# Projection to the queries and keys of differential attention, in both layers, by Strassen's seven half products

## The reference

```python
p = h @ w_in[l][:, diff columns]                     # 768 columns: q, k, v
q, k, v = jnp.split(p, 3, axis=-1)                   # 256 each
q, k = rope_2d(q of latents), rope_2d(k of latents)  # context tokens stay unrotated
amap = softmax(q1 k1 * scale) - lam * softmax(q2 k2 * scale)
o = amap @ v
```

## Time and profile before

| | us |
|---|---|
| median of 3 runs (2094.13 to 2097.17) | 2095.87 |
| the profiled execution | 2094.3 |
| its span | 2092.2 |
| TensorE busy (matmul) | 1942.3 (93%) |
| VectorE busy | 721.6 (34%) |
| ScalarE busy | 519.1 (25%) |

### The profile page before, as it was taken

The page is one execution under the profiler, slowest core; times in us unless marked ns, Lnnn a source line. Parts: engine busy times, 40 slices in busy tenths (PEclk is TensorE's granted clock), DMA queues, the critical chain, the costliest instruction groups (busy, mean ns, idle before and its releaser), DMA issues. The chain is left out here.

```text
span 2092.2 us, 25952 instructions
## 1 busy us (share of the span) xinstructions
PE 1942.3 (93%) x10858; PEld 934.4 (45%) x10858; DVE 721.6 (34%) x1335; ACT 519.1 (25%) x1020; POOL 186.9 (9%) x216
## 2 busy tenths in 40 slices
PE   5998999989989999999999999999898998888886
PEld 2656565544433333333334866655445333232222
DVE  2258565372431110111113476563624111111113
ACT  4146552452300000000003255524321100000012
POOL 1300000120011111212012000001100000000000
PEclk9999999999999999999999999999999999999999
DMA  9520304222289999999999223024419999999996
GB/s 351 147 81 1 141 1 152 90 105 96 82 343 401 393 399 395 394 401 393 402 395 301 111 82 141 1 90 153 165 61 357 395 408 408 408 409 409 409 409 261
DMA packets 164805, 530.64 MB, mean 254 GB/s; under 512 B 11016, under 2 KB 19538, under 8 KB 164690
## 3 DMA queue, kind: packets, MB, share of 16 engines
q1 hardware_dynamic: 149344, 489.49, 60.0%
q0 software_dynamic: 15120, 39.43, 6.1%
q10 hardware_dynamic: 226, 0.07, 0.0%
HBM read 507.98 MB, written 20.97 MB: 253 GB/s over the span
## 5 line engine op out<-in xcount | busy, mean ns | idle before, releaser
L3267 PE MATMUL ps<-ring,arena 128*64 128x512 f32 x1040 | 233.2, 597 | 13.6 <-DMA ring<-in_w_up 8.8
L3267 PE MATMUL ps<-arena 128*64 128x512 f32 x720 | 165.0, 604 | 3.6 <-DMA arena<-in_w_gate 3.2
L3267 PEld LDWEIGHTS ps<-ring,arena 128*64 128x64 f32 x1040 | 72.1, 137 | 161.6 <-issue 141.3
L3093 PE MATMUL ps<-ring,arena 128*128 128x512 f32 x320 | 141.6, 597 | 1.0 <-ACT arena L1442 0.6
L2366 DVE TENSOR_TENSOR arena<-arena,ps 128x512 f32<-128x512 f32 x32 | 22.0, 688 | 280.1 <-ACT arena L1487 280.1
L3316 PE MATMUL ps<-ring,arena 128*64 128x512 f32 x496 | 112.4, 596 | 5.8 <-DMA ring<-in_w_down 5.8
L2476 PE MATMUL ps<-arena,ring 128*128 128x256 f32 (+1 forms) x384 | 110.4, 447 | 2.5 <-DMA ring<-in_w_in 2.5
L1487 ACT ACTIVATE arena<-ps 128x512 f32<-128x512 f32 x32 | 19.1, 597 | 373.4 <-PE ps L3267 373.4
L3316 PE MATMUL ps<-arena 128*64 128x512 f32 x432 | 97.9, 595 | 5.2 <-DMA arena<-in_w_down 4.5
L1066 ACT ACTIVATE arena<-ps 128x768 f32<-128x768 f32 (+6 forms) x111 | 79.9, 724 | 88.0 <-PE ps L2494 45.3
L3267 PEld LDWEIGHTS ps<-arena 128*64 128x64 f32 x720 | 50.4, 139 | 107.0 <-issue 100.3
(11 more groups left out here) (417 smaller groups left out, 2821.8 us busy)
## 6 DMA issues: line engine op xcount, KB each, us to landing
ring<-in_w_up SPq DMA_DIRECT2D x33, 2048.0 KB, 14.7
ring<-in_w_gate SPq DMA_DIRECT2D x32, 2048.0 KB, 21.1
ring<-in_w_down SPq DMA_DIRECT2D x30, 2048.0 KB, 23.0
ring<-in_ada_w SPq DMA_DIRECT2D x24, 2048.0 KB, 9.9
arena<-in_w_down SPq DMA_DIRECT2D x19, 2048.0 KB, 23.2
arena<-in_w_gate SPq DMA_DIRECT2D x18, 2048.0 KB, 22.5
arena<-in_w_up SPq DMA_DIRECT2D x12, 2048.0 KB, 13.6
ring<-in_w_in SPq DMA_DIRECT2D x6, 2048.0 KB, 14.0
```

Of the source, the lines that this page charges most:

```text
L3093: ins = mm(o[:, hf * 512:(hf + 1) * 512], mix, wo[hf][:, k, :], start=k == 0, stop=k == KD - 1)
L3267: ins = mm(px[0][hf * 64:hf * 64 + 64, col:col + 512], xl[e % 2][:, at:at + CAP_L], w[c][:, hf * 512:hf * 512 + 512], start=b + c == 0, st ...
```

## The change

The four blocks are taken as two pairs, `p` = 0 with blocks 0 and 2 (a query block and a key block, 256 channels apart), `p` = 1 with blocks 1 and 3. Tokens are halved (384 and 384 in layer 0, 256 and 256 in layer 1), features too. For each pair there are seven half products of four feature blocks each. In this document they are numbered as they are issued, with a for pair 0 and b for pair 1:

1. first weights' half, first features, by first tokens; copied out by ScalarE
2. the same with the second features, into the same place once that copy is done
3. weight sum `SQ[1]` by token sum `TQ[1]`
4. `SQ[2]` by `TQ[2]`, onto the same place, once VectorE has taken product 3 (sums 11 and 12)
5. `SQ[0]` by `TQ[0]`
6. plain weights by `TQ[3]`
7. `SQ[3]` by plain tokens, in the place of 5 (sums 14 and 17)

The order is 1a 1b 2a 2b 3a 3b 4a 4b, 5a 6a 7a, 5b, the turn of block 2, 6b 7b, the turn of block 0; then the values, with the turns of blocks 3 and 1 behind the first (or only) values' job. VectorE makes eight sums of inputs first (four of tokens, four of weights), then sums results as products come, six to a pair. The rotations go in the order 2, 0, 3, 1: block 2's before pair 1 is finished, the other three behind it. ScalarE scales query blocks in place in SBUF. The first scores wait for two rotated blocks where they waited for three. Job numbers and tiles are as before.

```diff
+        def half_counts(l, conv):
+            return (10 * (2 * l + conv), (QK_SUMS + CONV_SUMS) * l + conv * QK_SUMS, 8 * l + conv * (4 if l else 6))
+        def qk_ready(l, m):
+            _, sums0, out0 = half_counts(l, 0)
+            if l and m >= 2:
+                return S["half_sums"], sums0 + (15 if m == 2 else 18)
+            return S["half_out"], out0 + ((3, 4)[m] if l else (4, 6, 3, 5)[m])
...
-                for m in range(4):
-                    j, scale = jb("qk") + m, DQ ** -0.5 if m < 2 else 1.0
-                    act.wait_ge(*J.filled(j))
-                    ins = act.activation(QK[:, m, CTX:TOK], J.tile(j)[:, CTX:TOK], ACT.Copy, scale=scale)
+                products0, sums0, _ = half_counts(l, 0)
+                _, _, EQ, _ = qk_sums_homes(l)
+                for p in range(2):
+                    act.wait_ge(S["half_products"], products0 + p + 1)
+                    act.activation(EQ[p], J.tile(jb("qk") + 2 * p)[:, 0:qk_half(l)], ACT.Copy).then_inc(S["half_out"], 1)
+                for m in (2, 0, 3, 1):
+                    scale = DQ ** -0.5 if m < 2 else 1.0
+                    if m < 2:
+                        act.wait_ge(*J.freed(jb("qk") + 2 * m + 1))
+                        ins = act.activation(QK[:, m, CTX:TOK], QK[:, m, CTX:TOK], ACT.Copy, scale=scale)
+                    elif l == 0:
+                        act.wait_ge(S["half_sums"], sums0 + (15 if m == 2 else 18))
                     if l == 0:
-                        ins = context_heads_out(QH if m < 2 else KH, m % 2, J.tile(j)[:, 0:CTX], scale)
-                    ins.then_inc(*J.free(j))
+                        ins = context_heads_out(QH if m < 2 else KH, m % 2, QK[:, m, 0:CTX], scale)
+                    if m < 2 or l == 0:
+                        ins.then_inc(S["half_out"], 1)
...
+                qk_sum(TQ[0], qk_rows(0, 1), qk_rows(0, 0), ALU.subtract)
+                qk_sums_done(1)
+                qk_sum(TQ[1], qk_rows(4, 1), TQ[0], ALU.subtract)
+                dve.wait_ge(ring_full[n4 % RING], ring_turns(n4) * 16)
+                qk_sum(SQ[0], qk_weights(1, 0), qk_weights(1, 4))
+                qk_sums_done(3)
+                qk_sum(SQ[1], SQ[0], qk_weights(0, 0), ALU.subtract)
+                qk_sum(SQ[2], qk_weights(0, 0), qk_weights(1, 0), ALU.subtract)
+                qk_sum(TQ[2], qk_rows(4, 1), qk_rows(0, 1), ALU.subtract)
+                qk_sums_done(4)
+                qk_sum(SQ[3], qk_weights(0, 4), SQ[1], ALU.subtract)
+                qk_sum(TQ[3], qk_rows(4, 0), TQ[1], ALU.subtract)
+                for p in range(2):
+                    dve.wait_ge(S["half_out"], out0 + p + 1)
+                    dve.wait_ge(S["half_products"], products0 + 3 + p)
+                    qk_sum(qk_out(p, 0), EQ[p], qk_tile(p, 0, 0))
+                for p in range(2):
+                    dve.wait_ge(S["half_products"], products0 + 5 + p)
+                    qk_sum(EQ[p], EQ[p], qk_tile(p, 0, 1))
+                for p in range(2):
+                    qk_sums_done(11 + p)
+                    dve.wait_ge(*J.filled(jb("qk") + 2 * p))
+                    TT(UQ[p], EQ[p], qk_tile(p, 0, 1), ALU.add).then_inc(*J.free(jb("qk") + 2 * p))
...
+                def qk_late(p):
+                    dve.wait_ge(*J.freed(jb("qk") + 2 * p))
+                    dve.wait_ge(S["half_products"], products0 + 7 + 2 * p)
+                    qk_sum(qk_out(2 + p, 1), UQ[p], qk_tile(p, 1, 0))
+                    qk_sum(EQ[p], EQ[p], qk_tile(p, 1, 0))
+                def qk_early(p):
+                    dve.wait_ge(S["half_products"], products0 + 8 + 2 * p)
+                    qk_sum(qk_out(2 + p, 0), UQ[p], qk_tile(p, 1, 1))
+                def qk_last(p):
+                    qk_sums_done((14, 17)[p])
+                    dve.wait_ge(*J.filled(jb("qk") + 2 * p + 1))
+                    TT(qk_out(p, 1), EQ[p], qk_tile(p, 1, 0), ALU.add).then_inc(*J.free(jb("qk") + 2 * p + 1))
+                qk_late(0)
+                qk_early(0)
+                qk_last(0)
+                qk_late(1)
+                for i, m in enumerate((2, 0, 3, 1)):
+                    if i == 1:
+                        qk_early(1)
+                        qk_last(1)
+                    dve.wait_ge(*qk_ready(l, m))
                     lat = QK[:, m, CTX:TOK]
                     TT(rope_t[0], lat, kc(K_COS, SEQ), ALU.mult)
                     j = jb("rot") + m
                     dve.wait_ge(*J.filled(j))
...
-                    pe.wait_ge(*J.freed(jb("qk") + m))
+                    pe.wait_ge(*qk_ready(l, m))
...
+                def qk_product(p, i, hf, a, b, k0=None):
+                    o = J.tile(jb("qk") + 2 * p + i)[:, 512 * hf:512 * hf + n]
+                    for k in range(4):
+                        if k0 is not None:
+                            h_ready(k0 + k)
+                        ins = mm(o, a[:, k, :], b[:, k, :], start=k == 0, stop=k == 3)
+                    return ins
+                def of_qk_pair(x, p):
+                    return SQ[x][:, :, P * p:P * p + P]
+                for p in range(2):
+                    pe.wait_ge(*J.empty(jb("qk") + 2 * p))
+                    qk_product(p, 0, 0, qk_weight(p, 0, 0), qk_rows(0, 0), 0 if p == 0 else None).then_inc(S["half_products"], 1)
+                for p in range(2):
+                    pe.wait_ge(S["half_out"], out0 + p + 1)
+                    qk_product(p, 0, 0, qk_weight(p, 0, 4), qk_rows(4, 0), 4 if p == 0 else None).then_inc(S["half_products"], 1)
+                pe.wait_ge(S["half_sums"], sums0 + 4)
+                for p in range(2):
+                    qk_product(p, 0, 1, of_qk_pair(1, p), TQ[1]).then_inc(S["half_products"], 1)
+                for p in range(2):
+                    pe.wait_ge(S["half_sums"], sums0 + 11 + p)
+                    qk_product(p, 0, 1, of_qk_pair(2, p), TQ[2]).then_inc(*J.fill(jb("qk") + 2 * p))
+                for p in range(2):
+                    pe.wait_ge(*J.empty(jb("qk") + 2 * p + 1))
+                    qk_product(p, 1, 0, of_qk_pair(0, p), TQ[0]).then_inc(S["half_products"], 1)
+                    if p:
+                        quarter_turned(2)
+                    qk_product(p, 1, 1, qk_weight(p, 1, 4), TQ[3]).then_inc(S["half_products"], 1)
+                    pe.wait_ge(S["half_sums"], sums0 + (14, 17)[p])
+                    qk_product(p, 1, 0, of_qk_pair(3, p), qk_rows(4, 1)).then_inc(*J.fill(jb("qk") + 2 * p + 1))
+                quarter_turned(0)
                 w = arrived(wb + 5)
                 wv = w
                 if l:
                     token_major(jb("v"), w[:, :, 0:256], range(CT, CT + 2), 256, 256)
                     quarter_turned(3)
+                    quarter_turned(1)
                     pe.wait_ge(*J.freed(jb("kc")))
                     pe.wait_ge(*J.freed(jb("vc")))
                 else:
                     token_major(jb("v"), w[:, :, 0:256], range(0, 4), 256, 256)
                     quarter_turned(3)
+                    quarter_turned(1)
                     token_major(jb("v") + 1, w[:, :, 0:256], range(4, 6), 256, 256)
                     pe.wait_ge(*J.freed(jb("v") + 1))
-                pe.wait_ge(*w_.next(S["qk_roped"], 3))
+                pe.wait_ge(*w_.next(S["qk_roped"], 2))
```

More of the change, by code:

```diff
@@ L599, in xr, with qk_half, qk_sums_homes @@
             return X[:, at:at + n]
+        QK_SUMS, CONV_SUMS = 18, 22
+        def half_counts(l, conv):
[5 more added lines that the diff above has]
+            return S["half_out"], out0 + ((3, 4)[m] if l else (4, 6, 3, 5)[m])
+        def qk_half(l):
+            return (TOK - query_tiles(l)[0] * P) // 2
+        def qk_sums_homes(l):
+            n = qk_half(l)
+            th = [view(x, k=4) for x in (ar(a0, 4 * n), ar(a0 + 4 * n, 4 * n), X[:, 4 * TOK:4 * TOK + 4 * n],
+                                         X[:, 4 * TOK + 4 * n:4 * TOK + 8 * n])]
+            sw = [view(ar(a2 + 1024 + i * 1024, 1024), k=4) for i in range(3)] + [view(ar(a0 + 8 * n if l else 21504, 1024), k=4)]
+            e = a1 + 4 * TOK + (512 if l else 0)
+            return th, sw, [ar(e + p * n, n) for p in range(2)], [ar(e + (2 + p) * n, n) for p in range(2)]
         HT = TOK // 2
@@ new lines, in qk_weights, with qk_sum, qk_out, qk_tile @@
+                def qk_weights(half, k0):
+                    return ringv(n4)[:, k0:k0 + 4, 256 * half:256 * half + 256]
+                def qk_sum(to, x, y, op=ALU.add):
+                    TT(to, x, y, op).then_inc(S["half_sums"], 1)
+                def qk_out(m, half):
+                    return QK[:, m, c0 + half * n:c0 + half * n + n]
+                def qk_tile(p, i, hf):
+                    return J.tile(jb("qk") + 2 * p + i)[:, 512 * hf:512 * hf + n]
+                if l:
+                    for b in range(4):
+                        dve.wait_ge(*J.freed(jb("hl") + b))
+                    dve.wait_ge(s_xst, 16 * nq)
@@ new lines, in _, with qk_weight, qk_rows @@
```

(10 more changed lines are left out.)

23 lines of the change are left out of this document (10 added, 13 removed).

## The result

| | before | after |
|---|---|---|
| median | 2095.6 (4 executions) | 2111.88 (4, from 2108.27 to 2113.92) |
| the profiled execution | 2094.3 | 2113.68 |
| its span | 2092.2 | 2111.5 |
| granted clock, mean of the span | 0.988 | 0.982 |
| VectorE busy | 721.6 | 753.0 |

The ratio is 1.0076, with a 95% interval from 1.0058 to 1.0094: slower by 16.3 us. The forecast said slower, 2104.9, with a range to 2109.5; the direction is right, the time lies outside the range. Seven half products for eight save work, and the kernel pays for it with holes and with clock.

A forecast was written before the change was run, and what follows sets the result against it. TensorE's stream was taken as the bound at the projection, if nothing else came late. Products and holes gave +0.7 and +5.7, low clock +2.6: +9.0 on a median of 2095.9, hence 2104.9 us, range 2098.5 to 2109.5.

The forecast's parts named there:

- The products and the stream: Projection in both layers: 14 half products for four blocks save 5.2 us in layer 0 and 3.4 in layer 1.
- The holes: TensorE waits before values, their second part, product 4a and first scores: 1.5 and 4.3 us; 0.3, 2.1, 2.4 and 4.3.
- The sum of +6.4: First scores later by 0.7 us in layer 0 and 5.7 in layer 1, saved products and holes together, without low clock.
- The clock behind the long holes: Half clock behind the 4.3 us hole of each layer, costing 1.3 us each, within bounds of 0 and 1.6.
- rival 3: All four holes bring low clock, also those of 2.1 and 2.4 us in layer 1: +12.8, 2108.7 us; chance 15%.
- +9.0: Whole kernel: +6.4 from products and holes plus 2.6 for low clock, if all holes of this length pay.
- My row of 2.45 us: Trace row at 42.7 us: half clock behind a 2.45 us hole, read as evidence that the 4.3 us holes lower the clock.
- the clock's term of the sum: Low clock behind the two 4.3 us holes, one in each layer, adds 2.6 us to +6.4.
- 1 (stream alone, -6.5): TensorE's stream alone decides, turned tiles being free in time before values and scores: 6.5 us faster, 2089.4; chance 5%.
- 2 (holes, no low clock): The holes in both layers cost +6.4 us, with no low clock behind them: 2102.3; chance 20%.
- 4 (later work takes part back): Behind layer 1's scores, half of 6.4 us is lost in existing slack, leaving +3: 2099; chance 12%.

The follow-up runs named there:

- the shifted kernel: Kernel before the change plus three unread multiplications ahead of the values in layer 0, moving later work without a hole; 2099.56 us, ratio 1.0016.
- the version without holes: Changed kernel with turned tiles reordered and, in layer 1, block 3's turn ahead of the values and two input sums later; 2090.58, then 2097.48 us.

## Why the prediction was right and wrong

**The products and the stream: right.** Product pairs stand 5.16 us apart in layer 0 (53.55 to 58.71) and single ones 1.73 in layer 1 (1191.38 to 1193.11), for 2 x 2.58 and 1.73. The last turn before the values ended at 81.1 for 81.2.

**The holes: right.** Named were 1.5 and 4.3 in layer 0; 0.3, 2.1, 2.4 and 4.3 in layer 1. Measured: 1.15 and 4.07; 0.19, 1.81, 1.85 and 4.31, each ended by the instruction named. Without the low clock behind the hole the values' second part (7.76 us to the scores) would have put the scores at 110.0; 110.3 was forecast. Layer 1's stretch grew by 5.55, forecast 5.7. The sum of +6.4 is 5.9 by the trace. That the tiles are the cause of the holes before the values, their second part and the scores is shown by the kernel that changes the tiles alone; that the wait before product 4a is one of VectorE's order, by the kernel that moves two input sums.

**The clock behind the long holes: right in kind, small in size.** I took 1.3 each; with the holes filled 1.7 and 1.6 came back. The three holes of 1.15 to 1.85 us had no low clock behind them in the traces read here: rival 3 falls. Holes of 4.07 to 4.31 fell each time, in layer 0 as well as in layer 1. The rule of the Trainium skill (TensorE: Matmul & The Clock Gate, section Why this matters for your kernels), that idle gaps between bursts send the engine back to its lower clock, agrees with the trace there, and its +9.0 was nearer than +6.4. My row of 2.45 us is weaker than I read it: in the 13 traces the hole ahead of the first product is 2.27 to 2.56 us long, and half clock follows in eleven and not in two (2.27 and 2.31), so near this length the length alone does not tell.

**The step that failed is the clock's term of the sum, +2.6 and no more.** I counted low clock only where a new hole stands, and took the rest of the kernel's low stretches as unchanged. The two holes cost 3.3. The granted clock over the whole span fell from 0.988 to 0.982, and most of that stands elsewhere: in the profiled execution, 19.3 us longer, one stretch of 13.7 us at half clock near 233 us costs 6.3 (the same in each of the four traces that have it) and a longer low stretch near 1468 us another 1.6. The delay at 1441 us (1.1) and the scattered 1 us are in no term either. Beyond the holes (5.9) and the clock right behind them (3.3) the median has 7.1 us for which the sum has no term. The long stretch is not the whole of it, since the execution without it took 2109.64.

**The agreement of one execution is luck.** The changed kernel's execution with the granted clock of the kernel before (0.987) took 2105.00, and I had forecast 2104.9. But it gained 4.1 us against the trace before in places that the forecast does not name (the start and near 1600 us) and lost some 5.4 in others (435.8, 473.3, 1441 and 1463 us). The nine others lie at 2108.27 to 2120.03, most of them above the range's upper end of 2109.5. Three executions of the kernel before (2094.13 to 2097.17) were too few to tell how far the granted clock spreads a time: 20 more of them lie from 2088.44 to 2100.02.

**The rivals.** 1 (stream alone, -6.5): not in this kernel, but its condition, the turned tiles free in time, is what the reordered kernels set up, and there the scores come earlier by 5.0 to 6.2 in layer 0 and the stretch of layer 1 is 2.5 shorter, without a measured gain in the whole. 2 (holes, no low clock): against it both rows behind the holes, with 0.50. 3: above. 4 (later work takes part back): no; from layer 1's scores to the end the kernel lost 4.6 us more, 1.6 of it in the low stretch right behind them.

**What stays open** is why the clock falls near 233 us and at the other places where it came and went. Near 233 us it is not a hole right ahead of it: TensorE was busy 7.00 of 7.00 us. It is not the shift alone: at that place the changed kernel's first trace stands 2.2 us late with the stretch, its third and the shifted kernel 2.1 late without it, and ten executions of the latter kept 0.986 to 0.988. It showed in three of five traces that have the changed order in both layers (holes filled or not), in one of two of the version without holes, and in none of the kernel before, of either layer alone (three traces), of the reordered tiles or of the shifted one. With one trace for most of these kernels, that is no proof that they are free of it.

## What to carry to other kernels

A buffer ring handed out by job number turns a reordering into waits: when steps are moved, write down for each tile who reads it last and who wants it next, down to the job that takes it fourth, before counting what the saved multiplications bring. Here a table of four numbers was worth 14 us, clock included, more than the 8.6 us that the algorithm was to save. And when an edit is worth less than half a per cent, read the granted clock beside each time: what looks like a gain of 5 us in one set of executions (2090.58) was none in the next, on another chip (2097.48).

## What the hardware showed that I had not expected

- TensorE can be granted 1.2 of its 2.4 GHz with no idle time ahead: 13.7 us from 233.0, with 24 instructions and 7.00 us busy in the 7 us ahead of it. The rule of the Trainium skill on idle gaps (TensorE: Matmul & The Clock Gate, section Why this matters for your kernels) does not cover this stretch.
- The same program had it in two traces (2113.68 and 2114.94) and not in two others (2109.64 and 2105.00). A hole of 2.3 us, too, was followed by half clock in some traces and not in others.
- Useless multiplications in a hole paid on the spot: 3.60 us of them into a hole of 4.07 and one of 4.31 brought back 1.7 and 1.6 us. In layer 0's trace 1.3 of the 1.7 was lost again by 140 us, to a low stretch that was longer than without them.
